# Projection of a hybrid attention block: splits before results, squares a tile ahead, three places for rotation rows

## The chip, the cores and the metric

The kernel runs on one core of one Trainium2 chip. The metric is the device time of one execution in microseconds (us). Two executions of it are told apart when their medians differ by more than the spread of the runs, which is about 0.1% here.

## The reference, cut to what matters

One encoder layer on 2048 tokens of width 1024, in float32. The part at hand is its beginning:

```python
h = rmsnorm(x, g_norm_mix[l])
proj = h @ w_in[l]                      # 1024 x 2304
qa, ka, va, qb, kb, vb = jnp.split(proj, split_at, axis=-1)
qb = partial_rope(qb.reshape(b, s, SWA_HEADS, HEAD_DIM), pos)
kb = partial_rope(kb.reshape(b, s, SWA_KV_HEADS, HEAD_DIM), pos)
oa = neighbourhood_attention(qa, ka, va, na_rpb[l]).reshape(b, s, A_WIDTH)
ob = windowed_gqa_sink(qb, kb, vb, swa_sink[l]).reshape(b, s, B_WIDTH)
o = jnp.concatenate([rmsnorm(oa, g_out_na[l]), rmsnorm(ob, g_out_swa[l])], axis=-1)
x = x + o @ w_out[l]
# a SwiGLU feed-forward with its own norm, and a final norm, follow
```

## The kernel before, in words

Each float32 factor of a product is split into a high and a low part in the format of the fast matmul, and a product is made of three matmuls (high by high, high by low, low by high). The projection runs in two stages, attention and the feed-forward follow.

In the first stage, 16 tiles of 128 tokens are loaded (three buffers), squared and summed by ScalarE, normalised by VectorE into one buffer, transposed on TensorE (turn_tile, 8 small matmuls) and multiplied with the values' columns (value_step, 24 matmuls). ScalarE copies the turned tile's high half out (turn_hi), VectorE makes the low half (turn_lo). For every pair of tiles sums of quarters are formed (turn_copy on ScalarE, turn_sums on VectorE) in a stage buffer hs of seven slices; for the second half of the tokens SyncE stores hs to DRAM (store_sums), and the operands are loaded from there later.

In the second stage the other columns are made with a scheme of seven products in place of eight: 14 groups g (7 column groups for each half b of the tokens) of seven products j, 98 in all, each of 12 matmuls. Step n = 7 g + j. The weights of a group arrive in one of two buffers (load_raw, issued by GpSimd); VectorE forms four sums of them, and ScalarE and VectorE split each product's weights into a ring of six (pair_hi, pair_lo), six steps ahead. ScalarE copies three of the seven banks out (evacuate), VectorE adds others onto them (join). Each group gives four results; ScalarE makes the high and VectorE the low part in one of three stages (result_hi, result_lo), and SyncE stores both. Group 1 of each half is first rotated by VectorE with cosine and sine rows loaded by SyncE (rope, load_rope), and one result of groups 1 and 2 takes a spare buffer. The second half's seven operands are loaded by SyncE (load_op) and split on both engines (split_hi, split_lo) from step 24 on. Eight tiles of output weights are loaded, split and stored along the way (load_out_weights, out_weights_hi, out_weights_lo, store_out_weights).

Nothing schedules this at run time: every engine runs its own list in program order, and semaphores make it wait. So an instruction that waits holds up all that stands behind it on its engine, transfers of SyncE's queue too. The order on each engine is written by hand in the loops over t (tiles) and n (steps), with tables such as HI_AT (the step of a group at which a result is handled), SPLIT_AT and OUT_AT. TensorE needs for product n its weights, and for j = 2, 4 and 5 that ScalarE has copied the bank filled two products before; for j = 6 that VectorE's join of j = 4 is done.

At the end SyncE loads masks and bias rows (load_near), and the first queries, keys and values of attention (first_loads); GpSimd forms biases from masks and rows (make_bias).

## Time and profile before

| | |
|---|---|
| median of 3 runs | 2266.8 us (2265.73 to 2267.71) |
| the profiled execution | 2267.85 us, its span 2266.0 us |
| TensorE busy | 2166.6 us, 96% |
| VectorE busy | 1565.9 us, 69% |
| ScalarE busy | 1012.7 us, 45% |
| GpSimd busy | 243.7 us, 11% |
| mean granted TensorE clock | 0.983 of full speed |

The times of the profile are microseconds from the span's start. PE is TensorE, PEld its weight loads, DVE VectorE, ACT ScalarE, POOL GpSimd, SPq SyncE's queue of transfers. L853 is a line of the kernel. In brackets or behind a bar stands how long an engine was idle before an instruction, and what ended that.

### The profile page before, as it was taken

The page shows a single profiled execution, that of the slowest core. Times are in us where ns is not written, and L with a number is a line of the kernel's source. Part 1 is how long each engine was busy: PE and PEld are TensorE (multiplying, and loading weights), DVE is VectorE, ACT ScalarE, POOL GpSimd, SP SyncE. Part 2 cuts the span into 40 slices and gives each one's busy share as a digit, 9 for nine tenths or more (in the row PEclk, how much of TensorE's full clock was granted, in tenths as well). Part 3 has the DMA queues.
Part 4 walks back from the last instruction along what each step waited for, and adds up shares of the span by engine and source line. Part 5 has one row for each costly group of instructions (what it writes and reads, how often), then busy time and mean ns, then how long its engine had stood idle before and what let it go on. Part 6 is the DMA issues. An engine that isn't in the chain of part 4 may idle for free.

```text
span 2266.0 us, 33068 instructions
## 1 busy us (share of the span) xinstructions
PE 2166.6 (96%) x11168; PEld 1787.7 (79%) x11168; DVE 1565.9 (69%) x2892; ACT 1012.7 (45%) x1967; POOL 243.7 (11%) x275
## 2 busy tenths in 40 slices
PE   7888988969999999999999999999999999999998
PEld 5677766758888888888888888888888888888887
DVE  5466676649988868777666666866666678665676
ACT  5443443448889944344333334433333334131333
POOL 2234100036400000001211111100000000000000
PEclk9989998989999999999999999999999999999999
DMA  6666676899985356665555557623232276353544
GB/s 196 186 192 196 194 243 225 276 246 259 243 219 172 110 190 211 241 219 171 190 172 190 172 190 251 222 89 121 89 121 89 103 287 235 112 181 110 178 152 157
DMA packets 267558, 419.34 MB, mean 185 GB/s; under 512 B 15242, under 2 KB 157074, under 8 KB 260896
## 3 DMA queue, kind: packets, MB, share of 16 engines
q1 hardware_dynamic: 254736, 378.20, 52.2%
q0 software_dynamic: 10240, 30.48, 4.5%
q10 hardware_dynamic: 2448, 8.91, 1.3%
q8 instruction: 79, 1.29, 0.2%
q14 instruction: 55, 0.45, 0.1%
HBM read 264.70 MB, written 156.04 MB: 186 GB/s over the span
## 4 chain that ended last, share of the span: by engine, by line
PE 80%; DVE 7%; DMA 5%; issue 3%; ACT 3%; SPq 1%; DVEq 0%; ACTq 0%
PE late_psum L2334 11%; PE late_psum L2336 11%; PE late_psum L2335 11%; PE late_psum L2360 6%; PE late_psum L2361 6%; PE late_psum L2362 6%; PE late_psum L1278 4%; PE late_psum L1255 3%; PE late_psum L1676 3%; PE late_psum L1678 3%; PE late_psum L1677 3%; PE late_psum L853 2%; PE late_psum L855 2%; PE late_psum L854 2%; PE late_psum L1243 2%
## 5 line engine op out<-in xcount | busy, mean ns | idle before, releaser
L2334 PE MATMUL late_psum<-ff_h,ff_ring 128*128 128x512 f32 x1232 | 479.6, 389 | 1.3 <-DVE ff_acts L2195 1.2
L2336 PE MATMUL late_psum<-ff_h,ff_ring 128*128 128x512 f32 x1232 | 479.3, 389 | 0.0
L2335 PE MATMUL late_psum<-ff_h,ff_ring 128*128 128x512 f32 x1232 | 479.3, 389 | 0.0
L2334 PEld LDWEIGHTS late_psum<-ff_h,ff_ring 128*128 128x128 f32 x1232 | 231.2, 188 | 50.1 <-DVE ff_acts L2195 2.1
L2335 PEld LDWEIGHTS late_psum<-ff_h,ff_ring 128*128 128x128 f32 x1232 | 231.2, 188 | 48.0
L2336 PEld LDWEIGHTS late_psum<-ff_h,ff_ring 128*128 128x128 f32 x1232 | 231.2, 188 | 47.9
L2360 PE MATMUL late_psum<-ff_d,ff_a 128*128 128x512 f32 x616 | 240.1, 390 | 2.1 <-DVE ff_x L2253 1.4
L2362 PE MATMUL late_psum<-ff_d,ff_a 128*128 128x512 f32 x616 | 239.7, 389 | 0.0
L2361 PE MATMUL late_psum<-ff_d,ff_a 128*128 128x512 f32 x616 | 239.7, 389 | 0.0
L2253 DVE TENSOR_TENSOR ff_x<-late_psum,ff_x 128x512 f32<-128x512 f32 x224 | 153.3, 689 | 118.1 <-PE late_psum L2362 117.5
L2153 DVE TENSOR_TENSOR ff_ring<-ff_raw,ff_ring 128x512 fp32r<-128x512 f32 x176 | 130.1, 740 | 101.2 <-ACT ff_ring L2030 101.2
L1143 ACT ACTIVATE att_probs<-att_neg_scores,att_negmax 128x385 f32<-128x385 f32 (+4 forms) x256 | 161.2, 630 | 29.6 <-DVE att_negmax L1190 28.5
L2153 DVE TENSOR_TENSOR ff_ring<-ff_sums,ff_ring 128x512 fp32r<-128x512 f32 x132 | 96.9, 735 | 112.2 <-ACT ff_ring L2030 111.9
L2045 ACT CAST ff_a<-ff_a 128x768 fp32r<-128x768 f32 (+2 forms) x96 | 81.4, 877 | 205.6 <-DMA ff_a<-acts_scratch 205.5
L2030 ACT CAST ff_ring<-ff_raw 128x512 fp32r<-128x512 f32 x176 | 109.3, 622 | 136.9 <-PE late_psum L2336 135.9
L1255 PE MATMUL late_psum<-ident,att_probs 128*128 128x128 f32 (+1 forms) x816 | 133.2, 276 | 8.7 <-ACT att_probs_turned L1165 4.0
L1165 ACT COPY att_probs_turned<-late_psum 128x384 f32<-128x384 f32 (+2 forms) x256 | 124.6, 488 | 29.3 <-PE late_psum L1255 29.1
L2360 PEld LDWEIGHTS late_psum<-ff_d,ff_a 128*128 128x128 f32 x616 | 115.6, 188 | 27.9 <-issue 2.1
L2362 PEld LDWEIGHTS late_psum<-ff_d,ff_a 128*128 128x128 f32 x616 | 115.6, 188 | 23.9
L2361 PEld LDWEIGHTS late_psum<-ff_d,ff_a 128*128 128x128 f32 x616 | 115.6, 188 | 23.8
L2030 ACT CAST ff_ring<-ff_sums 128x512 fp32r<-128x512 f32 x132 | 81.5, 619 | 113.6 <-PE late_psum L2336 108.2
L1243 PE MATMUL late_psum<-att_k_stack,att_q_stack 128*128 128x384 f32 (+3 forms) x256 | 112.5, 439 | 19.4 <-issue 12.0
(204 smaller groups left out, 4125.8 us busy)
## 6 DMA issues: line engine op xcount, KB each, us to landing
acts_scratch<-ff_acts SPq DMA_DIRECT2D x22, 1792.0 KB, 7.5
ff_a<-acts_scratch SPq DMA_DIRECT2D x24, 960.0 KB, 5.3
ff_raw<-in_w_gate SPq DMA_DIRECT2D x44, 512.0 KB, 3.8
ff_raw<-in_w_up SPq DMA_DIRECT2D x44, 512.0 KB, 3.9
att_q_stack<-qk_scratch SPq DMA_DIRECT2D x64, 256.0 KB, 6.5
ff_d<-down_scratch SPq DMA_DIRECT2D x21, 768.0 KB, 6.8
proj_raw<-in_w_in POOLq DMA_DIRECT2D x14, 1024.0 KB, 8.6
ffn_in_scratch<-mix_h_stage SPq DMA_DIRECT2D x8, 1792.0 KB, 6.2
```

Of the source, the lines that this page charges most:

```text
L1143: nc.scalar.activation(pr[:, i, lo:hi], sn[:, i, lo:hi], ACT.Exp, bias=negmax[:, i:i + 1], scale=-1.0, accum_out=total[:, i:i + 1]).then_i ...
L1243: pe.matmul(out, q, kind.keys(k_st[:, e, 0, :], t), start=True, stop=False)
L1255: last = pe.transpose(tp[0:rows, u % 2, j * P:(j + 1) * P], pr[:, i, c0 + j * P:c0 + j * P + rows], ident[:])
L2030: nc.scalar.copy(ff.ring[m % TURNS][:, 0], weight_of(m)).then_inc(w_hi_done, 1)
L2153: nc.vector.tensor_tensor(ff.ring[m % TURNS][:, 1], weight_of(m), ff.ring[m % TURNS][:, 0], ALU.subtract) \
L2253: nc.vector.tensor_tensor(to, down_bank(e, j), to, ALU.add).then_inc(added, 1)
L2334: pe.matmul(out_bank, whi[:, k], hhi[:, :, k], start=(k == 0 and not onto), stop=False, skip_group_check=onto)
L2335: pe.matmul(out_bank, whi[:, k], hlo[:, :, k], start=False, stop=False, skip_group_check=onto)
L2336: last = pe.matmul(out_bank, wlo[:, k], hhi[:, :, k], start=False, stop=(k == 3), skip_group_check=onto)
L2360: pe.matmul(bank, hi, dhi, start=(i == 0 and not onto), stop=False, skip_group_check=onto)
L2361: pe.matmul(bank, hi, dlo, start=False, stop=False, skip_group_check=onto)
L2362: last = pe.matmul(bank, lo, dhi, start=False, stop=(i == n - 1), skip_group_check=onto)
```

## The change

It changes the order of work in the projection on all engines but TensorE, and moves three pieces of it to other engines. The arithmetic is the same.

- First stage: ScalarE's square is its own step, done a tile ahead, and so are mean and reciprocal on VectorE. Root and normalised tile come first in each turn of the loop. The stage buffer hs is stored in four transfers instead of one, each as soon as its slices are there; ScalarE waits only for the slices that it writes (parts_stored), VectorE for its own (h_stored). The first operands and three weight pairs are split a tile or two earlier.
- Second stage: within a step ScalarE splits weights and operands ahead of results. Results are handled one to two steps later, their low halves one step after the high ones.
- Rotation rows have three places of their own; the three first are loaded at once, the last by ScalarE into the place of the first.
- Five operand loads of the second half are issued by ScalarE, from step 42 on, and its splits stand at other steps.
- GpSimd forms the weight sums of groups 7, 8 and 9; the others stay on VectorE, two of them earlier.
- Output weights come every five steps from 53 on, instead of every four from 59.
- Bias rows and the first mask are loaded at steps 78, 83 and 87, the two other masks at 97 behind the first loads of attention, which are issued at steps 91, 93 and 94. Biases of the first kind wait for their own rows alone. ScalarE waits in attention, ahead of its fifth step, for the last store of stage 2 (last_stage_stored).

```diff
-    SPLIT_AT_TILE = {13: (0, 2), 14: (0, 3), 15: (0, 4)}
-    SPLIT_AT = {0: (0, 6), 24: (1, 1), 31: (1, 0), 45: (1, 2), 46: (1, 3), 47: (1, 4), 49: (1, 5), 51: (1, 6)}
+    LATE_OPS, OP_SLOTS = PER_G * HALF_GROUPS - PER_G - 2, range(2, SEVEN)
+    SPLIT_AT_TILE = {12: (0, 2), 13: (0, 3), 14: (0, 4), 15: (0, 6)}
+    PAIR_AT_TILE = {11: 0, 12: 1, 13: 2}
+    SPLIT_AT = {26: (1, 1), 33: (1, 0), 46: (1, 2), 48: (1, 3), 49: (1, 4), 51: (1, 5), 52: (1, 6)}
+    SUMS_BY_POOL, SUMS_AT = (7, 8, 9), {1: 2}
+    PAIRS_AT = {n: (n + RING,) for n in range(PRODUCTS - RING)}
+    PAIRS_AT.update({0: (4, 5, 6), 1: (), 2: (), 3: (7,), 4: (8, 9), 5: (10, 11)})
...
-    HI_AT = {ROPED: (2, 5, 6, 8), VALUES: (1, 6, 5, 9)}
-    ROPE_AT = (1, 4, 5, 7)
-    order = sorted(((PER_G * g + HI_AT.get(kind_of(g), (1, 4, 5, 6))[i], g, i) for g in range(G) for i in range(4)))
+    HI_AT = {ROPED: (3, 6, 7, 9), VALUES: (3, 7, 6, 9)}
+    ROPE_AT = (2, 5, 6, 8)
+    ROPE_SLOT = (0, 1, 2, 0)
+    order = sorted(((PER_G * g + HI_AT.get(kind_of(g), (3, 5, 6, 7))[i], g, i) for g in range(G) for i in range(4)))
...
     def store_sums(u):
+        sp.wait_ge(h_copied, 2 * u + 2)
+        sp.dma_start(sums_dram[5, :, u - 4], hs[:, 5]).then_inc(parts_stored, 16)
         sp.wait_ge(h_summed, 4 * (u + 1))
-        sp.dma_start(sums_dram[:, :, u - 4].rearrange("o p c -> p o c"), hs[:]).then_inc(h_stored, 16)
+        sp.dma_start(sums_dram[2:5, :, u - 4].rearrange("o p c -> p o c"), hs[:, 2:5]).then_inc(h_stored, 16)
+        sp.dma_start(sums_dram[6, :, u - 4], hs[:, 6]).then_inc(h_stored, 16)
+
+    def store_parts(u):
+        sp.wait_ge(h_copied, 2 * u + 1)
+        sp.dma_start(sums_dram[0:2, :, u - 4].rearrange("o p c -> p o c"), hs[:, 0:2]).then_inc(parts_stored, 16)
...
+    def load_rope(eng, b, i):
+
+        side, half = SIDES[i]
+        if i == 3:
+            eng.wait_ge(roped, 4 * b + 1)
+        elif b == 0:
+            eng.wait_ge(v_done, NT)
         else:
-            sp.wait_ge(prod_done, HOME_FREED[o])
-        sp.dma_start(hc[:, o, 1].bitcast(F32), sums_dram[o].rearrange("p q c -> p (q c)")).then_inc(h_in[o], 16)
+            eng.wait_ge(prod_done, PER_G * HALF_GROUPS)
...
-    OUT_AT = {59 + 4 * k: k for k in range(KT)}
+    OUT_AT = {53 + 5 * k: k for k in range(KT)}
...
+            if g - 1 in SUMS_BY_POOL:
+                last_weight_sum(pool, g - 1)
+            if g in SUMS_BY_POOL:
+                first_weight_sums(pool, g)
+                middle_weight_sum(pool, g)
...
             nc.scalar.copy(v_st[:, t % 2, :], mm[:, t % 4, :]).then_inc(tok_done, 1)
+            if t + AHEAD < NT:
+                root(t + AHEAD)
+            if t + 5 < NT:
+                load_x(t + 5)
             if t + 2 < NT:
                 turn_hi(t + 2)
-                if t + 5 < NT:
-                    load_x(t + 5)
                 turn_copy(t + 2)
-            if t + AHEAD < NT:
-                root(t + AHEAD)
+            if t + AHEAD + 1 < NT:
+                square(t + AHEAD + 1)
...
             if n < PRODUCTS:
                 evacuate(n)
+            if n - LATE_OPS in OP_SLOTS:
+                load_op(act, n - LATE_OPS)
+            for m in PAIRS_AT.get(n, ()):
+                pair_hi(m)
+            if n in SPLIT_AT:
+                split_hi(*SPLIT_AT[n])
             for r, g, i in results_at(n):
                 result_hi(r, g, i)
-            if n + RING < PRODUCTS:
-                pair_hi(n + RING)
-            if n in SPLIT_AT:
-                split_hi(*SPLIT_AT[n])
+                if kind_of(g) == ROPED and i == 0:
+                    load_rope(act, g // HALF_GROUPS, 3)
...
         for t in range(NT):
+            if t + AHEAD < NT:
+                normed_tile(t + AHEAD)
             if t + 2 < NT:
                 turn_lo(t + 2)
                 if t % 2:
                     turn_sums((t + 2) // 2)
-            if t + AHEAD < NT:
-                normed_tile(t + AHEAD)
+            if t + AHEAD + 1 < NT:
+                mean_tile(t + AHEAD + 1)
...
-            if n + RING < PRODUCTS:
-                pair_lo(n + RING)
-            if n in SPLIT_AT:
-                split_lo(*SPLIT_AT[n])
-            for r, gg, i in results_at(n):
+            for r, gg, i in results_at(n - 1):
                 result_lo(r, gg, i)
             for gg, i in ropes_at(n):
                 rope(gg, i)
-            if j == 2 and g + 1 < G:
-                weight_sums(g + 1)
-            if j == 4 and g + 1 < G:
-                last_weight_sum(g + 1)
+            for m in PAIRS_AT.get(n, ()):
+                pair_lo(m)
+            if n in SPLIT_AT:
+                split_lo(*SPLIT_AT[n])
```

## Rows read from the trace of the kernel before

**Rows 1.** Page, part 1: busy time of TensorE, share of the span.

```profile
PE 2166.6 (96%) x11168; PEld 1787.7 (79%) x11168; DVE 1565.9 (69%) x2892; ACT 1012.7 (45%) x1967; POOL 243.7 (11%) x275
```

**Rows 2.** Stretches: PE, PEld, DVE, ACT, POOL busy us; clock, DMA share, GB/s.

```profile
14.30:146.70 132.40, 114.80 (x496) 92.38 (x497) 70.76 (x114) 59.75 (x109) 31.73 (x63) 0.91 0.57 173
146.70:462.10 315.40, 282.36 (x1193) 228.54 (x1191) 206.62 (x301) 134.22 (x215) 52.43 (x85) 0.95 0.71 228
462.10:503.00 40.90, 20.20 (x131) 16.71 (x131) 19.00 (x71) 18.69 (x49) 16.20 (x15) 0.75 1.06 241
503.00:2266.00 1763.00, 1745.29 (x9336) 1446.91 (x9334) 1264.10 (x2400) 792.91 (x1583) 140.86 (x106) 1.00 0.55 176
```

**Rows 3.** TensorE's waits, 14.3 to 146.7: us in total, times, longest.

```profile
PE late_psum L792 <- DVE x_normed L657: 16.9, 9, 3.4
```

**Rows 4.** Timeline of TensorE: start, duration, instruction, idle before.

```profile
22.38 1.09 PE L792 MATMUL late_psum<-ident,x_normed 128*128 128x128 f32 x8 [0.42 <-ACT proj_h_stage L491]
...
54.24 1.09 PE L792 MATMUL late_psum<-ident,x_normed 128*128 128x128 f32 x8 [1.94 <-DVE x_normed L657]
...
60.66 1.05 PE L792 MATMUL late_psum<-ident,x_normed 128*128 128x128 f32 x8
```

**Rows 5.** Timeline of all engines, 110 to 114 us.

```profile
110.35 1.01 ACT L489 COPY proj_h_stage<-late_psum 128x1024 f32<-128x1024 f32 x1 [3.53 <-DMA proj_in_scratch<-proj_h_stage]
...
111.47 1.29 DVE L632 TENSOR_TENSOR x_turned<-late_psum,x_turned 128x512 fp32r<-128x512 f32 x2 [6.91 <-ACT proj_h_stage L489]
...
113.28 1.28 DVE L657 SCALAR_TENSOR_TENSOR x_normed<-x_tile,rstd,g_mix_rows 128x1024 f32<-128x1024 f32 x1 [0.27 <-ACT rstd L498]
```

**Rows 6.** TensorE's waits, 146.7 to 462.1.

```profile
PE late_psum L853 <- ACT proj_c L540: 22.5, 5, 8.1
PE late_psum L853 <- issue: 6.5, 3, 3.9
PE late_psum L853 <- DVE proj_c L697: 2.1, 3, 1.0
PE late_psum L853 <- DVE proj_ring L671: 1.9, 1, 1.9
```

**Rows 7.** Timeline of TensorE within a product.

```profile
149.44 0.39 PE L853 MATMUL late_psum<-proj_h_first,proj_ring 128*128 128x512 f32 x1
...
150.12 0.39 PE L853 MATMUL late_psum<-proj_h_first,proj_ring 128*128 128x512 f32 x1
```

**Rows 8.** Timeline of SyncE's queue and VectorE around the first rotation.

```profile
192.03 1.01 SPq L294 DMA_DIRECT2D rope_rows<-in_rope  x2
197.76 0.01 DVE L711 LOAD_MASK_SELECT rope_swapped<-proj_c  x1 [6.63 <-DMA rope_rows<-in_rope]
```

**Rows 9.** Timeline of ScalarE: split of an operand.

```profile
303.88 1.89 ACT L513 CAST proj_h_second<-proj_h_second 128x2048 fp32r<-128x2048 f32 x1
```

**Rows 10.** Groups by line and shape: busy us, mean ns, idle before.

```profile
L667 DVE TENSOR_TENSOR proj_h_second<-proj_h_second 128x2048 fp32r<-128x2048 f32 x7 | 16.0, 2292 | 7.0 <-ACT proj_h_second L513 7.0
...
L1121 POOL TENSOR_TENSOR bias<-near_mask,rel 128x512 f32<-128x512 f32 x24 | 32.3, 1379 | 2.0 <-DVE att_negmax L1190 2.0
```

**Rows 11.** Timeline while GpSimd forms bias rows, 460 to 463 us.

```profile
459.94 3.38 POOL L1121 TENSOR_TENSOR bias<-near_mask,rel 128x384 f32<-128x384 f32 x3
...
461.07 1.39 DVE L727 TENSOR_TENSOR stage_lo<-proj_c,stage_hi 128x512 fp32r<-128x512 f32 x1 [0.78 <-ACT stage_hi L568]
...
462.96 0.69 DVE L729 SCALAR_TENSOR_TENSOR stage_lo<-late_psum,stage_hi 128x512 fp32r<-128x512 f32 x1 [0.49 <-ACT stage_hi L568]
```

**Rows 12.** Timeline at the seam to attention.

```profile
474.17 0.63 PE L1243 MATMUL late_psum<-att_k_stack,att_q_stack 128*128 128x352 f32 x1 [11.96 <-issue]
...
499.07 0.76 PE L1243 MATMUL late_psum<-att_k_stack,att_q_stack 128*128 128x480 f32 x1 [5.18 <-DMA att_q_stack<-qk_scratch]
```

**Rows 13.** Line 308, the seven operand loads of 1 MB: time to landing.

```profile
DMA to landing us min/median/max: 5.9/10.0/14.0
```

**Rows 14.** Timeline of ScalarE: output weights.

```profile
370.83 1.15 ACT L576 ACTIVATE w_out_parts<-w_out_raw,g_out 128x1024 fp32r<-128x1024 f32 x1 [5.59 <-DMA w_out_raw<-in_w_out]
```

More of the change, by code:

```diff
@@ L257, in results_split, with last_stage_stored, near_arrived @@
         eng.wait_ge(res_lo, LOWS)
-    def near_arrived(eng):
-        eng.wait_ge(near_in, 16 * len(near_parts))
+    def last_stage_stored(eng):
+        eng.wait_ge(stored[2], max(v for r, v in stored_by.items() if r % STAGES == 2))
+    def near_arrived(eng, kind):
+        if kind == 0:
+            eng.wait_ge(near_in, 48)
+        else:
+            eng.wait_ge(near_masks_in, 32)
     def out_weights_stored(eng):
@@ L348, in store_out_weights, with first_loads, later_loads @@
         sp.dma_start(out_dram[k], out_parts[:].bitcast(F32)).then_inc(out_stored, 16)
-    OUT_AT = {59 + 4 * k: k for k in range(KT)}
+    OUT_AT = {53 + 5 * k: k for k in range(KT)}
     def load_near(part):
         dst, src = near_parts[part]
-        sp.dma_start(dst, src).then_inc(near_in, 16)
-    def first_loads(att):
-        sp.wait_ge(prod_done, PRODUCTS - 6)
-        for slot in range(STAGES):
-            sp.wait_ge(stored[slot], max(v for r, v in stored_by.items() if r % STAGES == slot and order[r][1] < G - 2))
-        att.load_q(att.near, 0, 0)
-        sp.wait_ge(prod_done, PRODUCTS - 4)
-        att.load_k(att.near, 0, 0)
-        att.load_k(att.near, 0, 1)
-        sp.wait_ge(prod_done, PRODUCTS - 3)
-        for half in range(2):
-            sp.wait_ge(v_stored[half], 32 * NT)
-            sp.wait_ge(v_stored_by_pool[half], 32 * NT)
-        att.load_v(att.near, 0, 0)
-        att.load_v(att.near, 0, 1)
+        sp.dma_start(dst, src).then_inc(near_in if part < 3 else near_masks_in, 16)
+    def first_loads(att, turn):
+        sp.wait_ge(prod_done, PRODUCTS - SEVEN + (1, 3, 4)[turn])
+        if turn == 0:
+            for slot in range(STAGES):
+                sp.wait_ge(stored[slot], max(v for r, v in stored_by.items() if r % STAGES == slot and order[r][1] < G - 2))
+            att.load_q(att.near, 0, 0)
+        if turn == 1:
+            att.load_k(att.near, 0, 0)
+            att.load_k(att.near, 0, 1)
+        if turn == 2:
+            for half in range(2):
+                sp.wait_ge(v_stored[half], 32 * NT)
+                sp.wait_ge(v_stored_by_pool[half], 32 * NT)
+            att.load_v(att.near, 0, 0)
+            att.load_v(att.near, 0, 1)
+    def later_loads(att):
         att.load_k(att.near, 0, 2)
         att.load_q(att.near, 0, 1)
-    def later_loads(att):
         att.load_v(att.near, 0, 2)
@@ L409, in sync @@
                 sp.wait_ge(table_made, 16 * (2 + 8 * NAH))
-                for part in range(3):
-                    load_near(part)
-            if n == 91:
+                load_near(0)
+            if n in (83, 87):
+                load_near({83: 1, 87: 2}[n])
+            for r, g, i in results_at(n - 1):
+                store_result(r, g, i)
+            if n == 91:
+                first_loads(att, 0)
+            if n == 93:
+                first_loads(att, 1)
+            if n == 94:
+                first_loads(att, 2)
+            if n == 97:
                 out_weights_stored(sp)
@@ L584, in scalar @@
         load_x(2)
-        root(0)
-        root(1)
+        for n in range(2):
+            square(n)
+            root(n)
         turn_hi(0)
@@ L592, in scalar @@
         load_x(4)
+        square(2)
         root(2)
@@ L740, in vector @@
         dve.wait_ge(table_loaded, 1)
-        normed_tile(0)
-        normed_tile(1)
+        for n in range(2):
+            mean_tile(n)
+            normed_tile(n)
         turn_lo(0)
@@ L776, in vector @@
                 rope(gg, i)
[L777 to L780 removed]
+            for m in PAIRS_AT.get(n, ()):
+                pair_lo(m)
+            if n in SPLIT_AT:
+                split_lo(*SPLIT_AT[n])
+            if g + 1 < G and g + 1 not in SUMS_BY_POOL:
+                if n == SUMS_AT.get(g + 1, PER_G * g):
+                    first_weight_sums(dve, g + 1)
+                if j == 2:
+                    middle_weight_sum(dve, g + 1)
+                if j == 5:
+                    last_weight_sum(dve, g + 1)
             if n - 2 in OUT_AT:
@@ L1112, in make_bias @@
                 pool.wait_ge(shifted, UNITS * r + 8 * freed)
-            elif kind == 1:
-                proj.all_read(pool)
-                proj.results_split(pool)
+            else:
+                proj.near_arrived(pool, kind)
+                if kind == 1:
+                    proj.all_read(pool)
+                    proj.results_split(pool)
             for e in range(2):
```

161 lines of the change are left out of this document (81 added, 80 removed).

## Prediction

> **What bounds the kernel now.** I read the page's engine shares first: TensorE is busy 96% of the span [rows 1]. A change on other engines can only pay where TensorE idles or is granted half its clock, so I read the busy time by stretch next [rows 2]. After 503 us TensorE is busy 1745.3 of 1763.0 us at full clock; nothing touched by the diff can gain there. Before it lie three stretches: 132.4 us of normalising, turning and the first values, 315.4 us of products, and 40.9 us at the seam to attention. The third view gives TensorE's waits in each [rows 3, 6], the fourth the pace when it doesn't wait [rows 4, 7].
>
> First stretch. Two turns that start at 54.24 and 60.66 with no wait between them give 6.42 us for a turn and its 24 matmuls. From the turn at 22.38 there are 14 such pairs and one value step of 24 matmuls at 0.227 us (5.45): 22.4 + 14 x 6.42 + 5.45 = 117.7 us, where products start now at 146.7. So 29.0 us are lost. Waits for the normalised tile explain 16.9 [rows 3]. The other 12.1 are clock: the stretch has a mean grant of 0.91 [rows 2], that is 2.4 GHz with spells at 1.2 GHz behind the longer waits, and 0.09 x 132.4 is 11.9.
>
> Products. Three matmuls take 0.68 us [rows 7], 12 take 2.72, 98 products 266.8, and 16 small transposes about 2: 268.7. The stretch takes 315.4, so 46.7 are lost: 33.0 in waits [rows 6] and 13.7 at half clock (by the grant, 0.05 x 315.4 = 15.8 at most).
>
> Seam. TensorE ends its products at 462.1, waits 12.0 us and later 5.2, and is past the last long wait at 499.07 [rows 12]; DMA share is 1.06 meanwhile [rows 2].
>
> **Part 1, norms and squares.** The chain stands in [rows 5]. ScalarE waits 3.53 us for the store of the stage buffer, copies (1.01), and only then does VectorE make its low halves (1.29), after which mean, reciprocal and root follow and the normalised tile starts at 113.28, done at 114.56; TensorE has waited 3.4 for it. The change squares a tile ahead, puts root and normalised tile first after the value copy, and lets the copy wait only for its own two smaller stores. The normalised tile then needs: the turn before it read (about 1.1 us behind the value step), then 1.28. That is 2.4 of 6.5 us until the next turn, so the wait goes. What comes later instead are the low halves and sums: value copy and turned halves (three at about 0.55, half the 1.01 of the wide copy), the copy (1.0) and the low halves (1.3) end some 4.8 us after the value step, behind a turn of 1; they are wanted at 7.6, when the next turn and the next value step are over. VectorE's work for two tiles is 2 x 1.28, eight operations at 0.65 (two take 1.29 [rows 5]) and 0.6 of small ones: 8.4 of 12.8 us. The slack of 2.8 us is also what hides a late store. I take 27 of the 29.0; bounds 20 (a third of the copies still wait for a store) and 29. The first product waited 1.9 us for a weight half; four operands and three pairs are now split a tile earlier, and that wait is part of the next sum.
>
> **Part 2, order in the products.** Now ScalarE's result copy stands before its weight halves, so a result that isn't joined or rotated stops the ring. Moving results to steps 3, 5, 6, 7, one step behind the join, and VectorE's low halves to the step after, removes that. What it costs is a later store: the shortest reuse of a stage goes from high half at step 3 to high half at step 7, leaving 4 x 2.72 less about 4.4 for lows and issue, 6.5 us for the store to land, and then ScalarE can still be 3.8 us late before TensorE misses a bank copy. No row shows how long these stores take. Loads of 1 MB took 5.9 at best, 10.0 in the median and 14.0 at worst [rows 13]; a pair of stores is half a megabyte, so I take under 6.5 and cost it at nothing. At 10.0 it would still be covered, at 14.0 not.
>
> **Part 3, rotation rows.** The second pair of table rows is issued at 192.03 and VectorE stands 6.63 us until 197.76 [rows 8], and TensorE's wait of 8.1, the longest of its kind [rows 6], follows. The same happens in the second half. Three buffers are now loaded before any rotation, and only the fourth use is reloaded, five products (13.6 us) ahead, by ScalarE. Both waits go.
>
> **Part 4, operands and weight sums.** A split is 1.9 us on ScalarE [rows 9] and 2.29 on VectorE [rows 10]. Between steps 46 and 52 VectorE has 5 splits x 2.2, 7 pairs, 3 joins and 4 lows x 0.6: 19.4 us of work in seven products of 19.05. Before, four weight sums (4 x 0.6) came on top for the same steps. GpSimd takes them for three groups: 12 sums of 512 columns at 1.38 us [rows 10], 16.6 us of an engine with nothing else to do there; each group's four fit in its 19 us. By my schedule VectorE finishes the last split about when product 55 wants it, and the join before it is 0.7 late. So the three waits of 6.5 in total [rows 6] shrink to about 1.5, clock included 2. The five loads of 1 MB are on ScalarE's queue, first at step 42, one every 2.72 us (its engine loses nothing: issues run beside its copies). With stores and one weight load about 8 MB move in 27 us. A load wanted 10.9 us after issue against a median of 10.0 and a longest above it is thin; I add 2 us [rows 13].
>
> GpSimd's sums have one price more. While GpSimd formed bias rows, a VectorE subtraction with both inputs in SBUF took 1.39 us; the next, of the same width but with a PSUM input, took 0.69 [rows 11]. Twelve such delays of 0.70 are 8.4 us, of 1.38 each 16.6; the offload saves 12 x 0.61 = 7.3. In the seven crowded steps five of them fall: 3.5 to 7 us late, of which most reaches the last two splits. I take 2.5.
> The Trainium skill, page "SBUF — State Buffer", section "Who interferes with whom", says that a VectorE instruction with two SBUF inputs and a GpSimd one that reads SBUF take turns, the later blocked for the whole instruction. The trace agrees as far as one delayed subtraction can; by the rule the sum would be at the upper bound (7 instead of 2.5), by the row at the lower.
>
> **Part 5, output weights.** ScalarE waited 5.59 us for a load two steps ahead of use [rows 14], and TensorE's waits of some 3 us stand behind such places. Loads now stand every five steps; at the tight ones about 6.6 us remain. I leave 1.5 us.
>
> Products together: 46.7 lost now, less 2 + 2 + 2.5 + 1.5 = 8 left: gain 38.7, bounds 22 (half of it stays, because transfers are late) and 46.
>
> **Part 6, seam.** The first attention loads are issued at steps 91, 93 and 94 instead of behind step 95's store, the queries so about 13 us ahead of TensorE's end (step 91 and 2 to 3 us). But masks and three stores (2.8 MB) now go ahead of the later keys and queries. Volume decides: some 6.8 MB behind the end of products at 241 GB/s [rows 2] are 28 us, with the latency of the last 30, until the third query block, where it is 36.9 now [rows 12]. I take 6; bounds 0 and 12. The new wait of ScalarE in front of its fifth attention step is for a store issued 3 to 5 us after the end; behind it stand exponentials of later units, and cover is the wait for keys.
>
> **Sum.** 27 + 38.7 + 6 = 71.7. Profiled execution 2267.85 (span 2266.0), median 2266.8, 1.05 lower: 2266.8 - 71.7 = 2195, taken as 2196.
>
> **Rivals.**
> A. As summed: 2196, its own range 2184 to 2210. For it: each wait has a named cause that the new order takes out. Chance 0.60.
> B. Transfers become the bound. DMA share was 0.71 in the products; the same bytes in 275 us make 0.81, and with part 1 some stretches ask for 300 GB/s. Landings stretch, half of the products' gain goes: 2196 + 23 = 2219. Chance 0.18.
> C. GpSimd's sums block VectorE for whole instructions, splits late, 7 us and some clock: 2206. The rule of the Trainium skill quoted above leads here. Chance 0.12.
> D. The seam gives nothing: 2202. Chance 0.06.
> E. Slower than before: the later stores. If a pair of stores needs over 6.5 + 3.8 = 10.3 us, ScalarE holds TensorE once in each of 14 groups; to eat 71 us it must be 5.4 more, 15.7 us each. The 1 MB loads at their slowest are near that, pairs of 256 KB shouldn't be. 2270 or more: 0.02.
> Left over 0.02 for no visible change.
>
> **Chances and range.** Faster A to D, 0.96; same 0.02 (4.5 us, 0.2%, is about what a measurement of this kernel tells from nothing); slower 0.02. Below 2180 all bounds would have to be good at once; above 2222 lies a good third of B. Range 2180 to 2222.
>
> **What the profile would show.** Right: waits on the normalised tile gone and the first product near 118 to 121; no wait for rotation rows; grant near 1.00 in both stretches; products in 274 to 280 us; third query block 30 us behind. Wrong: VectorE subtractions of 1.4 to 2 us around GpSimd's sums with waits at products 54 and 55 (C); splits, output weights or result copies that wait for transfers (B); the third query block still 37 us behind (D); result copies that wait for stores in each group (E).

## The result and the profile after

The changed kernel takes 2212.92 us (median of four executions, 2211.68 to 2217.22) against 2266.27 for the kernel before on the same chip: ratio 0.977 [0.975, 0.979], 53.4 us faster, where 70.8 were forecast. Its profiled execution took 2214.03 us (span 2212.2, mean grant 0.991), 53.8 less than that of before. The page's first part and the busy time by stretch (columns as in [rows 2]):

```profile
PE 2147.7 (97%) x11168; PEld 1778.0 (80%) x11168; DVE 1566.8 (71%) x2880; ACT 1012.2 (46%) x1967; POOL 267.4 (12%) x287
```

```profile
14.30:115.90 101.60, 101.10 (x496) 84.54 (x497) 74.53 (x118) 61.16 (x111) 31.62 (x63) 1.00 0.71 226
115.90:409.40 293.50, 275.60 (x1193) 225.10 (x1191) 200.71 (x284) 131.60 (x212) 79.51 (x99) 0.98 0.75 241
409.40:446.80 37.40, 19.73 (x116) 15.99 (x116) 17.66 (x59) 17.05 (x43) 13.64 (x12) 0.68 1.05 272
```

Beside [rows 1, 2] this splits the gain. The first stretch shrank from 132.4 to 101.6 us (30.8; forecast 27), the products from 315.4 to 293.5 (21.9; forecast 38.7). The rest follows by the same pair of matmuls in both traces. (Attention works in units, eight to a block of queries: the ninth opens the second block, the seventeenth the third.) Those of the twenty-first unit of attention start 54.02 us earlier, first before, then after:

```profile
506.48 0.47 PE L1243 MATMUL late_psum<-att_k_stack,att_q_stack 128*128 128x480 f32 x1
452.46 0.47 PE L1299 MATMUL late_psum<-att_k_stack,att_q_stack 128*128 128x480 f32 x1
```

The profiled executions as wholes differ by 53.8. So the seam gave 54.0 - 30.8 - 21.9 = 1.3 (forecast 6). The waits of TensorE in the three stretches, answering to [rows 3, 6]:

```profile
PE late_psum L859 <- DVE v_w_lo L722: 0.5, 1, 0.5
PE late_psum L847 <- DVE x_normed L717: 0.3, 1, 0.3
...
PE late_psum L908 <- ACT proj_c L588: 7.8, 2, 6.9
PE late_psum L908 <- DVE proj_c L740: 6.2, 1, 6.2
PE late_psum L908 <- DVE proj_h_second L727: 2.2, 2, 1.6
PE late_psum L908 <- issue: 1.7, 2, 1.3
...
PE late_psum L1299 <- DMA att_q_stack<-qk_scratch: 7.8, 1, 7.8
PE late_psum L1299 <- issue: 6.1, 1, 6.1
PE late_psum L1299 <- DVE stage_lo L775: 3.5, 1, 3.5
```

Of the first stretch 0.8 us of waits is left, at full clock. Most of its turns come faster than the 6.42 us of [rows 4]:

```profile
21.53 1.09 PE L847 MATMUL late_psum<-ident,x_normed 128*128 128x128 f32 x8 [0.29 <-DVE x_normed L717]
27.95 1.04 PE L847 MATMUL late_psum<-ident,x_normed 128*128 128x128 f32 x8
34.29 1.03 PE L847 MATMUL late_psum<-ident,x_normed 128*128 128x128 f32 x8
```

The first two stand 6.42 apart, the next 6.34, and all later ones 6.33 to 6.37; the mean up to the turn at 104.12 is 6.35. The first starts 0.85 earlier than before: 21.53 + 14 x 6.35 + 5.45 = 115.9, where products start. The one pace of 6.42 here begins at a turn behind a wait (0.29), and so did the pair in the trace of before from which 6.42 was taken (1.94 at 54.24).

Among the products TensorE waits 17.9 us, in seven waits. Three of them, 0.60, 1.59 and 0.40, stand at the first products of the second half, which need its operands (2.6). One of 1.28, at 133.68, is at the first product on the last operand of the first half. No wait for rotation rows is left. The other 14.0 (6.93, the 0.89 some 11 us behind it, and 6.22) have one cause, seen in the timeline of SyncE's queue, ScalarE and TensorE:

```profile
284.53 1.50 SPq L349 DMA_DIRECT2D qk_scratch<-stage_hi  x1
286.07 0.93 SPq L349 DMA_DIRECT2D qk_scratch<-stage_lo  x1
286.62 0.39 ACTq L312 DMA_DIRECT2D rope_rows<-in_rope  x1
287.04 0.98 SPq L358 DMA_DIRECT2D w_out_raw<-in_w_out  x1
298.75 1.15 ACT L624 ACTIVATE w_out_parts<-w_out_raw,g_out 128x1024 fp32r<-128x1024 f32 x1 [10.06 <-DMA w_out_raw<-in_w_out]
...
304.61 0.63 ACT L616 ACTIVATE stage_hi<-proj_c 128x512 fp32r<-128x512 f32 x1 [3.20 <-DVE proj_c L762]
305.14 0.57 ACT L588 COPY proj_c<-late_psum 128x512 f32<-128x512 f32 x1
305.76 0.79 PE L908 MATMUL late_psum<-proj_h_second,proj_ring 128*128 128x512 f32 x1 [6.93 <-ACT proj_c L588]
306.36 0.63 PE L909 MATMUL late_psum<-proj_h_second,proj_ring 128*128 128x512 f32 x1
306.78 0.63 PE L910 MATMUL late_psum<-proj_h_second,proj_ring 128*128 128x512 f32 x1
...
362.58 1.15 ACT L624 ACTIVATE w_out_parts<-w_out_raw,g_out 128x1024 fp32r<-128x1024 f32 x1 [6.81 <-DMA w_out_raw<-in_w_out]
365.71 0.80 PE L908 MATMUL late_psum<-proj_h_second,proj_ring 128*128 128x512 f32 x1 [6.22 <-DVE proj_c L740]
```

Read it from the bottom of a block upward. The load of output weights is issued at 287.04, and ScalarE reaches the instruction that needs it at 288.7. The load is there at 298.75, 10.7 us after the issue ended, behind two pairs of stores and a table row. ScalarE works in order: while it stands, the weight halves and the copies of banks behind it stand too, VectorE's joins and rotations wait for those, and TensorE has nothing to do from 298.8. When the load is there, VectorE has to catch up first: ScalarE stands another 3.20 us for a rotated result, and only then copies the bank that TensorE waits for. The same begins with the wait that ends at 362.58.

The granted clock falls to 1.2 GHz inside each of the two waits and stays there for 6.8 us, of which 4.4 and 5.9 lie behind the wait. There matmuls start 0.43 us apart and not 0.227, which costs 2.2 and 2.9 us. (The expectation below counts the whole 6.8 us, 3.4 lost each; the part inside the wait costs nothing more.) So 14.0 + 5.1 = 19.1 of the 24.8 that this stretch (293.5) loses against 268.7. With the waits of 2.6 and 1.28 that makes 22.9; the other 1.9 go back to neither waits nor clock. The first edit below has as much (1.7) at full clock, so the base of 268.7 is some 2 us low.

The seam, in the timeline of SyncE's queue, ScalarE and TensorE, answering to [rows 12]:

```profile
401.79 6.05 SPq L1105 DMA_DIRECT2D att_k_stack<-qk_scratch  x8
...
415.07 1.25 SPq L372 DMA_DIRECT2D near_mask<-in_na_mask  x2
419.90 0.60 ACT L616 ACTIVATE stage_hi<-late_psum 128x512 fp32r<-128x512 f32 x1 [9.66 <-DMA qk_scratch<-stage_lo]
421.27 0.66 PE L1299 MATMUL late_psum<-att_k_stack,att_q_stack 128*128 128x352 f32 x1 [3.50 <-DVE stage_lo L775]
426.19 1.26 SPq L1095 DMA_DIRECT2D att_q_stack<-qk_scratch  x2
434.49 0.77 PE L1299 MATMUL late_psum<-att_k_stack,att_q_stack 128*128 128x480 f32 x1 [7.79 <-DMA att_q_stack<-qk_scratch]
```

The first unit starts 6.3 us behind the end of the products, against 12.1. But the last result copy waits 9.66 us for an older store to leave its stage buffer. That pair of stores is issued at 409.82 and 412.01, behind the early keys and values (401.79 to 409.8). The keys and queries of the next block are issued behind that result and behind the masks, at 422 to 427. The ninth unit starts 25.1 us behind the end of the products, where it was 21.7 (483.80), and the third query block 37.4 (446.83), where it was 37.0. That the seam gave 1.3 all the same is clock: before, the third block begins behind a wait of 5.18 [rows 12] and its first two units start 1.67 us apart; here it begins with no wait in front and they start 0.88 apart.

### The profile page after: what moved, and what is told of

The parts are those of the page before. It is cut to its first block, busy times and chain, and to the rows that moved or that the text cites. A ratio compares the mean times of both kernels' runs of the same rounds, so it can differ in the third digit from the quotient of the medians.

```text
span 2212.2 us, 33085 instructions
## 1 busy us (share of the span) xinstructions
PE 2147.7 (97%) x11168; PEld 1778.0 (80%) x11168; DVE 1566.8 (71%) x2880; ACT 1012.2 (46%) x1967; POOL 267.4 (12%) x287
## 3 DMA queue, kind: packets, MB, share of 16 engines
q8 instruction: 79, 1.29, 0.2%
## 4 chain that ended last, share of the span: by engine, by line
PE 86%; DVE 5%; DMA 4%; issue 2%; ACT 1%; SPq 1%; DVEq 0%; ACTq 0%
PE late_psum L2391 12%; PE late_psum L2392 12%; PE late_psum L2393 12%; PE late_psum L2417 6%; PE late_psum L2419 6%; PE late_psum L2418 6%; PE late_psum L1334 4%; PE late_psum L1311 4%; PE late_psum L908 3%; PE late_psum L909 3%; PE late_psum L910 3%; PE late_psum L1733 3%; PE late_psum L1735 3%; PE late_psum L1734 3%; PE late_psum L1299 2%
```

## The experiments

Each ratio is to the kernel before, run on the same chip; medians are of four executions, with rotation rows of five. The first four ran beside one another on one chip, then the next four on another, then the last four on a third, so times of different chips are best compared by their ratios. The end of the products is counted from here on from the start of their last matmul (409.18 in the changed kernel), 0.2 us earlier than above.

**Output weights used four steps behind their load.** Undoes the cause named above, and nothing else.

```diff
-            if n - 2 in OUT_AT:
-                out_weights_hi(OUT_AT[n - 2])
+            if n - 4 in OUT_AT:
+                out_weights_hi(OUT_AT[n - 4])
```
(and the same for the low halves on VectorE and the store on SyncE)

> The changed kernel, but each tile of output weights is split on ScalarE and VectorE (and stored) four steps behind its load instead of two. Theory T (too short a distance): ScalarE's waits for these loads, 10.06 and 6.81 us, and with them TensorE's waits of 6.93, 0.89 and 6.22 us and two spells at half clock of 6.8 us (3.4 us lost each) go: about 21 us, 2213 to 2192 us. Rival V (the transfers are too slow whatever the distance): the load still lands late or another wait takes its place, under 8 us gained, above 2205 us.

Measured: 2197.44 us (2197.39 to 2198.46), ratio 0.969 [0.968, 0.971], 70.4 less than before, where the changed kernel has 53.4. The kernel with weight sums on VectorE, no different from the changed one in time, took 14.1 us more on this chip, and the pair further down that ran on one chip differs by 13.2. So the edit is worth 13 to 17 us, nearer to theory T's 21 than to V's 8. The stretch of products by busy time, and what is left of ScalarE's waits for these loads:

```profile
116.20:391.50 275.30, 270.37 (x1192) 221.60 (x1191) 196.93 (x284) 131.94 (x212) 76.68 (x99) 1.00 0.79 256
```

```profile
ACT w_out_parts L624 <- DMA w_out_raw<-in_w_out: 3.9, 3, 2.0
```

In the changed kernel the row of ScalarE is 21.5 us, longest 10.1. The products take 275.3 us at full clock, 18.0 less; waits of 4.9 us are left of 17.9. About 1 us comes back at the seam (the twenty-first unit stands 44.4 behind the end of the products, not 43.3). The cause of the two long waits is thereby shown; its size is 18 us of the 19.1 in the stretch, and 1.1 and 0.2 us of waits are still there.

**Before, with the first stage alone.** Splits square and mean off, puts root and normalised tile first, stores the stage buffer in four.

```diff
+            if t + AHEAD < NT:
+                root(t + AHEAD)
...
-            if t + AHEAD < NT:
-                root(t + AHEAD)
+            if t + AHEAD + 1 < NT:
+                square(t + AHEAD + 1)
```

> The kernel before with the first stage of the change alone: squares, means and reciprocals a tile ahead, root and normalised tile first, the stage buffer stored in four parts. Theory: these parts alone take out all waits and half clock of the first stage, first product at about 116 us instead of 146.7, and the rest stays as it was: 30 us gained, 2236 us. Rival: the later stages were waiting for transfers that are now asked for more densely and give a part back: 10 to 20 us gained, 2247 to 2256 us.

Measured: 2237.81 us (2237.33 to 2239.21), ratio 0.987 [0.985, 0.989], a gain of 30.0. The first stretch and the products, and TensorE's longest group of waits among the products:

```profile
14.30:116.60 102.30, 100.93 (x497) 84.39 (x498) 69.22 (x114) 58.89 (x109) 31.63 (x63) 1.00 0.69 224
116.60:432.60 316.00, 282.70 (x1192) 228.95 (x1191) 207.84 (x301) 134.27 (x215) 52.04 (x84) 0.95 0.71 227
```

```profile
PE late_psum L877 <- ACT proj_c L550: 22.5, 4, 8.1
```

The theory's 2236 nearly came. The first stage's 30 us stand by themselves, without the earlier splits of operands and pairs, and the products neither gain nor lose by starting 30 us earlier.

**Before, with the three places for rotation rows alone**, all loaded by SyncE.

```diff
+    ROPE_SLOT = (0, 1, 2, 0)
...
-        for side, half in enumerate((0, 1) if turn == 0 else (1, 0)):
+        for i in ((0, 1, 2) if turn == 0 else (3,)):
```

> The kernel before with three places for the rotation rows alone (three loads ahead, the fourth behind the first rotation, all by SyncE). Theory: TensorE's waits of 8.1 and 7.7 us and the half clock behind them (6.8 and some 7 us of spells, half of it lost) go: 18 to 22 us gained, 2245 to 2248 us. Rival: in the second half splits and late operands hold the rotation anyway, only the first wait goes: 11 us gained, 2255 us.

Measured: 2257.28 us (2253.3 to 2259.28), ratio 0.995 [0.994, 0.997], a gain of 10.6. TensorE's waits for result copies in the products, the longest of them, and what ScalarE did ahead of it:

```profile
PE late_psum L858 <- ACT proj_c L542: 13.6, 6, 5.1
```

```profile
358.57 1.15 ACT L578 ACTIVATE w_out_parts<-w_out_raw,g_out 128x1024 fp32r<-128x1024 f32 x1 [6.04 <-DMA w_out_raw<-in_w_out]
360.24 0.79 PE L858 MATMUL late_psum<-proj_h_second,proj_ring 128*128 128x512 f32 x1 [5.14 <-ACT proj_c L542]
```

The wait of 8.1 us is gone. Where the one of 7.7 was, one of 5.14 stands, and it isn't for rotation rows: ScalarE stands 6.04 us for output weights. So does the second longest, 3.57 at 416.70, behind 6.49 us for another such load. The four others are 0.7 to 1.4. The places alone gave 10.8 us in the stretch (315.1 to 304.3). The time is the rival's (11), but what holds the second half is output weights and not operands: their loads were too late already in the kernel before.

**Weight sums back on VectorE.**

```diff
-    SUMS_BY_POOL, SUMS_AT = (7, 8, 9), {1: 2}
+    SUMS_BY_POOL, SUMS_AT = (), {1: 2}
```

> The changed kernel with all weight sums on VectorE, none on GpSimd. Theory S (the offload pays): VectorE has 19.4 us of work plus 2.4 us of sums in seven products of 19.05 us, the operand splits get later, TensorE's waits of 0.6, 1.6 and 0.4 us around the first second-half products grow by 3 to 6 us: 2216 to 2220 us. Rival L (what GpSimd's sums cost VectorE by blocking it is as much as they save): no difference beyond 2 us, 2211 to 2215 us.

Measured: 2211.57 us (2210.43 to 2212.42), ratio 0.975 [0.974, 0.977]: no difference from the changed kernel, rival L. The timeline of the changed kernel shows what each engine does to the other:

```profile
254.24 1.29 POOL L453 TENSOR_TENSOR proj_w_sums<-proj_raw 128x512 f32<-128x512 f32 x1 [7.17 <-DVE proj_ring L731]
254.44 3.24 DVE L727 TENSOR_TENSOR proj_h_second<-proj_h_second 128x2048 fp32r<-128x2048 f32 x1 [0.34 <-ACT proj_h_second L561]
255.61 3.22 POOL L455 TENSOR_TENSOR proj_w_sums<-proj_w_sums,proj_raw 128x512 f32<-128x512 f32 x1
257.60 1.78 DVE L773 TENSOR_TENSOR stage_lo<-proj_c,stage_hi 128x512 fp32r<-128x512 f32 x1
```

A split takes 3.24 us in place of 2.29 [rows 10], a subtraction 1.78 in place of 0.69, and GpSimd's own sum 3.22 in place of 1.29. The ends fit turns: the sum ends at 255.53, and 2.29 from there is 257.82, where the split ends at 257.68; 1.29 from 257.68 is 258.97, where the next sum ends at 258.83; 0.69 from there is 259.52, where the subtraction ends at 259.38. A group of VectorE from 150 to 290 us, first with GpSimd's sums, then (second fence) without:

```profile
L731 DVE TENSOR_TENSOR proj_ring<-proj_raw,proj_ring 128x512 fp32r<-128x512 f32 x28 | 21.7, 782 | 9.1 <-ACT proj_ring L573 9.1
```

```profile
L731 DVE TENSOR_TENSOR proj_ring<-proj_raw,proj_ring 128x512 fp32r<-128x512 f32 x28 | 19.0, 686 | 8.3 <-ACT proj_ring L573 8.3
```

That is 2.7 us; the seven splits take 17.0 and not 16.0, 1.0 more; the low halves of results, 21 in two groups, go from 684 and 683 ns to 823 and 804, another 2.8. So 6.5 us are lost to save 12 x 0.685 = 8.2, and GpSimd is busy for 22.2 us more (47.12 against 24.92 in the same stretch). The waits of TensorE for operand splits were 0.60, 1.59 and 0.40 with GpSimd, and 2.18 and 1.02 without.

**The last group's results two steps earlier.**

```diff
-    order = sorted(((PER_G * g + HI_AT.get(kind_of(g), (3, 5, 6, 7))[i], g, i) for g in range(G) for i in range(4)))
+    order = sorted(((PER_G * g + HI_AT.get(kind_of(g), (3, 5, 6, 7) if g < G - 1 else (1, 4, 5, 6))[i], g, i)
+                    for g in range(G) for i in range(4)))
```

> The changed kernel with the results of the last group alone handled at the steps of before (1, 4, 5, 6 instead of 3, 5, 6, 7), so that the store of its first result stands ahead of the attention loads in SyncE's queue. Theory Q (the last result waits 9.66 us for a stage whose store is queued behind 4 MB of attention loads, and the later keys and queries wait behind that result's own store): TensorE's wait of 3.5 us goes, later keys and queries are issued some 4.6 us earlier, the wait of 7.8 us shrinks: 4 to 8 us gained, 2205 to 2209 us. Rival W (the volume of transfers alone sets when the third query block is worked on): under 1.5 us, 2211 to 2213 us.

Measured: 2214.41 us (2212.34 to 2218.1), ratio 0.978 [0.976, 0.980]: no difference, rival W. TensorE's wait of 3.5 us is gone and the next one, for queries, took it over (7.79 before):

```profile
433.28 0.76 PE L1299 MATMUL late_psum<-att_k_stack,att_q_stack 128*128 128x480 f32 x1 [11.84 <-DMA att_q_stack<-qk_scratch]
```

**The first, fourth and fifth together** (output weights four steps behind, sums on VectorE, last results earlier).

> The changed kernel with three edits together: output weights used four steps behind their load, the last group's results at the steps of before, all weight sums on VectorE. If they add up (15.5 and 0 to 1.5 us measured for the first and third, 4 to 8 expected for the second): 2189 to 2194 us. If the seam is bound by volume: 2196 to 2198 us.

Measured: 2201.95 us (2199.96 to 2202.25), ratio 0.971 [0.969, 0.973], above both expectations and some 4.5 us more than the first edit alone on another chip, with intervals that overlap. The traces have the difference: the products take 278.3 us and not 275.3, and the twenty-first unit stands 45.5 behind them (44.4). In the products a wait of 2.3 us for a result copy is new, behind a result's high half that waited 5.25 us for its stage's store. At the seam the ninth unit stands 28.0 us behind (26.4). What each of the two added edits has in it wasn't taken apart.

**The same, with the keys and queries of the next blocks issued a step ahead of the last results.**

```diff
+            att.load_k(att.near, 0, 2)
+            att.load_q(att.near, 0, 1)
```
(in the loads of step 94, and no longer behind the last store)

> As the kernel with the three edits, and besides the third portion of keys and the second query block are loaded right behind the first values (step 94), ahead of the masks and of the last three results' stores. Theory Q: with a stage's store queued ahead the last result isn't held up, the ninth unit's wait for queries goes, but those stores land later: 2 to 5 us gained against the three edits. Rival W: the bytes up to the third query block are the same, no difference beyond 1.5 us; and if the last results' stores are held up behind the added 1.5 MB, the early units wait again and it is slower by 2 to 4 us.

Measured: 2203.51 us (2201.09 to 2205.45), ratio 0.973 [0.971, 0.975]: no gain, rival W. TensorE no longer waits for queries, but for turned probabilities, mainly twice (7.30 and 5.35 us). The first of the two goes back to a store, the second to masks:

```profile
416.05 0.48 ACT L1220 COPY att_probs_turned<-late_psum 128x384 f32<-128x384 f32 x1 [6.67 <-DMA qk_scratch<-stage_lo]
416.67 0.45 PE L1311 MATMUL late_psum<-ident,att_probs 128*128 128x128 f32 x1 [7.30 <-ACT att_probs_turned L1220]
419.79 1.27 POOL L1176 TENSOR_TENSOR bias<-near_mask,rel 128x512 f32<-128x512 f32 x1 [36.06 <-DMA near_mask<-in_na_mask]
```

ScalarE's first copy of turned probabilities stands behind the wait for the last store of stage 2, which the change put in front of its fifth attention step. In the changed kernel that wait is covered by the wait for queries; with queries early it stands open, 6.67 us, and TensorE behind it. The second, at 429.40, stands behind scores that waited for GpSimd's biases, and those for the masks, which are now last. Whichever of keys, queries, masks and results is sent last is the one waited for.

**The first edit with the old order within a step:** results ahead of weight halves on ScalarE, lows and stores in the same step, and the old steps.

```diff
-    HI_AT = {ROPED: (3, 6, 7, 9), VALUES: (3, 7, 6, 9)}
-    ROPE_AT = (2, 5, 6, 8)
+    HI_AT = {ROPED: (2, 5, 6, 8), VALUES: (1, 6, 5, 9)}
+    ROPE_AT = (1, 4, 5, 7)
...
```

> The changed kernel with output weights used four steps behind their load (2197.4 us measured), and the order of before within a step: results ahead of the weights' halves on both engines, at the steps of before (HI_AT, ROPE_AT), low halves and stores in the same step. Rotation places, operand loads and first stage stay as changed. Theory O (splits first is what keeps the ring full): TensorE's waits behind result copies that aren't joined or rotated come back, as the 1.0 to 5.1 us ones in the kernel with rotation places alone: 10 to 20 us slower, 2207 to 2217 us. Rival P (with rotation rows, operands and output weights in time the order costs nothing): within 3 us, 2195 to 2200 us.

Measured: 2212.73 us (2211.36 to 2215.04), ratio 0.977 [0.975, 0.979], 15.3 us more than the first edit (16.5 by the ratios), theory O. The products take 288.7 us and not 275.3, with these waits of TensorE:

```profile
PE late_psum L908 <- ACT proj_c L588: 8.8, 6, 2.2
PE late_psum L908 <- issue: 5.5, 3, 3.6
```

The six of the first line are for bank copies. The three of the second, 1.38, 3.65 and 0.43, stand at the first products of the second half, whose splits the old order puts behind results. So Part 2's order is worth some 15 us once rotation rows and output weights are in time.

**The changed kernel again, beside the three below.**

> The changed kernel itself, unaltered, on the chip on which the next three run, so that they have a common base. 2211 to 2215 us.

Measured: 2211.23 us (2210.44 to 2213.14), ratio 0.976 [0.974, 0.977].

**Output weights four steps behind, sums on VectorE.**

> The changed kernel with output weights used four steps behind their load and all weight sums on VectorE, the seam untouched. Theory L (GpSimd's sums save VectorE about what they cost it by blocking it): within 2 us of the kernel with the output weights alone, 2195 to 2199 us. Rival S (the offload pays once the output weights no longer hide it): 3 us or more slower, above 2200 us.

Measured: 2198.07 us (2198.02 to 2199.67), ratio 0.970 [0.968, 0.971], 13.2 us less than the changed kernel beside it and the same as the first edit, theory L. GpSimd's sums are worth nothing here either.

**Output weights every four steps, masks before the results.** This frees the end of the queue: the last two masks are loaded at step 88.

```diff
-    OUT_AT = {53 + 5 * k: k for k in range(KT)}
+    OUT_AT = {53 + 4 * k: k for k in range(KT)}
...
-            if n == 97:
+            if n == 88:
```
(and the weights used three steps behind their load)

> The changed kernel with output weights loaded every four steps from 53 on and used three steps behind their load, and with the two late masks (1.3 MB) loaded at step 88 instead of 97, ahead of the attention loads. Theory W (the seam takes as long as its transfers): 1.3 MB less behind the products' end at the 291 GB/s measured there are 4.5 us: TensorE is at its ninth unit some 21 us behind the end instead of 25 to 26, and with the output weights' 15 us 2193 us. Rival X (the same bytes crowd the last products instead: three steps are too short or result stores land late): waits of 3 us and more come back among the products, 2198 to 2206 us.

Measured: 2206.41 us (2205.8 to 2208.48), ratio 0.974 [0.972, 0.975], 4.8 us less than the changed kernel beside it, and short of theory W (2193): rival X. TensorE's waits among the products, then at the seam:

```profile
PE late_psum L908 <- DVE proj_c L740: 6.9, 1, 6.9
PE late_psum L908 <- ACT proj_c L588: 5.4, 3, 3.5
...
PE late_psum L1299 <- DMA att_q_stack<-qk_scratch: 4.5, 1, 4.5
PE late_psum L1299 <- DVE stage_lo L775: 2.7, 1, 2.7
```

The ninth unit now stands 18.4 us behind the products (25.0 in the changed kernel beside it) and the twenty-first 35.9 (42.9): the 7 us of the seam were there to be had. But the products take 292.3 us, against 290.8 beside it: at three steps, with a load every four, output weights are late again (ScalarE waits 5.88 us for one at 363.05).

**The same, with sums on VectorE, last results and next keys earlier.**

> As the kernel with the masks early, and besides the last group's results at the steps of before, the third keys and second queries at step 94 and all weight sums on VectorE. Theory W: with masks out of the way neither biases nor queries hold the ninth unit, TensorE is there 16 to 19 us behind the products' end: 2188 to 2192 us. Rival X: result stores queue behind more loads and hold the early units, no better than the masks alone, 2193 to 2203 us.

Measured: 2207.79 us (2204.01 to 2209.24), ratio 0.973 [0.972, 0.975]. That is above both expectations. The ninth unit is at 17.1 us, the twenty-first at 38.0 (35.9 without these edits): nothing more at the seam, and the products unchanged at 291.8. Here too ScalarE stands 5.01 us in front of that step for the last store of stage 2, and TensorE waits 5.70 behind it.

## Why the prediction was right and wrong

**In sum.** The forecast was 2196, the time 2213. It lies inside the range of 2180 to 2222, but outside the 2184 to 2210 of the case with a chance of 0.60: the range held because it reached to case B, not because the sum did. (B's 2219 is 23 more; half of the 38.7 of the products, as it says, would be 19.4 and 2215.) Of the 17.7 us of missing gain (71.7 less 54.0), the products lack 16.8 and the seam 4.7, and the first stage gave back 3.8. In the products Part 5 cost 17.6 more than priced and Part 4 3.9 less; the wait of 1.28 for the last operand of the first half and the base that is 1.9 low were in no term. The total missed by no more than Part 5 alone because Parts 1 and 4 were wrong the other way, by 3.8 and 3.9.

**Part 1 held.** 27 us were forecast and 30.8 came; 30.0 by the run with this part alone. The bound of 29 was too low: it took the pace of a turn (6.42) and the start at 22.38 from the trace of before as fixed. The start had a wait of 0.42 us for the stage buffer in front of it [rows 4]. The pace was read from a turn that stood behind a wait of 1.94, which costs some 0.07 us at its start; without waits a turn takes 6.35. (The 13.7 us that the working puts down to half clock in the products before are some 11 by the spacing of the matmuls; the rest is the base that is low.)

**Part 2 held, and is worth more than its price of nothing says.** No wait of TensorE among the products goes back to a later store, rival E's mechanism, in the changed kernel; ScalarE does wait for stages, 10.1 us in five waits, and that is covered; what goes back to a stage's store is the wait of 3.5 at the seam, behind a copy that stood 9.66 us. With the old order the first edit loses 15 us.

**Part 3 held as to these waits, but not as a gain of its own.** In the old order the places bring 10.6 us and not both long waits: where the second was, late output weights hold TensorE for 5.14.

**Part 4 held in cause, and less came.** Two terms of 2 and one of 2.5 were forecast; the three waits for the second half's operands come to 2.6 without half clock. Rival C was right about the duration of a blocked instruction and wrong about the end. In the Trainium skill, page "SBUF — State Buffer", section "Who interferes with whom", two such instructions take turns, and the later one is blocked for the whole of the other. The trace agrees, for a subtraction of 512 columns (1.78 us beside a sum, 0.69 alone), for a split of 2048 that starts 0.2 us behind a sum of 1.29 and ends 0.95 late, and for GpSimd's next sum, begun beside the split, which takes 3.22: each ends within 0.15 us of where it would by turns. The delays eat 6.5 of the 8.2 us that the offload saves. The predicted 2.5 us of loss by it isn't there; without GpSimd the waits for splits are 3.2 us, with it 2.6.

**Part 5 failed: "At the tight ones about 6.6 us remain. I leave 1.5 us".** This term measured 19.1 in the stretch, 18.0 of which went with the first edit. The working had the right place, and left about 6.6 us to a distance of two steps, which is 5.4 us of products, although the row beside it, a load two steps ahead of use, showed a wait of 5.59 [rows 14], and the 1 MB loads had a median of 10.0 [rows 13]. The load landed after 10.7, with two pairs of stores ahead of it, and ScalarE was at its instruction 0.7 us behind the issue. Of ScalarE's 10.06 us TensorE was covered for 3.1, of its 6.81 us at 362 for 0.6: weight halves, bank copies and high halves stand behind the one waiting instruction, and the joins and rotations of VectorE behind those. That is rival B in one place: "some transfers late", not the volume as such, for with four steps the products run at a DMA share of 0.79 and lose 7 us in all.

**Part 6 failed as rival D says: the seam gives next to nothing.** Volume decides, as the working has it, but the gain was counted for the loads that were moved earlier, and the end depends on the one that is sent last. The first unit came earlier (6.3 us behind the products, not 12.1), the ninth later (25.1, not 21.7). What is sent last sets it: with masks early the seam is 7 us shorter; with keys and queries early and masks late it isn't. TensorE's wait of 3.5 us was for a stage buffer, Part 2's later store met at the seam, and in no term here; taking it away gained nothing, since the wait for queries grew from 7.79 to 11.84. The new wait in front of the fifth attention step was priced at cover, and cover it has in the changed kernel. Where queries come early it has none: it then costs TensorE 7.30 and 5.70 us, which the timelines give as one reason why the two runs with early queries gained nothing at the seam. No run took that wait out.

**Open.** That half a megabyte needs 10.7 us when the DMA share over the stretch is 0.75 is in part the queue at that moment: the share is 0.96 from 285 to 291 us, with GpSimd's megabyte of weights (issued at 282.04), stores and table rows ahead, and 2.8 MB move between the issue and the landing. Why the share is only 0.53 from 292 to 297, with the load still on its way, wasn't settled. The output weights four steps behind together with early masks weren't tried; by the runs above that might be worth up to 7 us more, if the products stay at 275. Nor were early masks and queries without ScalarE's wait for the last store. Why the first, fourth and fifth edit together lose some 4 us was read from their timeline alone.

## What to carry to other kernels

A load that an in-order engine waits for needs a distance taken from landings in the queue as loaded there, if copies that free the matmuls' banks stand behind it: landings took about 10 us, two steps gave 5.4 and four give 10.9, and those two steps were worth 13 to 17 us. At a seam that is bound by volume, what paid was to send something before the crowd; moving one transfer past another only changed which was last. And additions moved from VectorE to GpSimd saved next to nothing here, where VectorE had two-input work in SBUF to do. Before a wait is put down to the kind that was expected there, look at what the releasing engine itself waited for: twice here it was another load or store.

## What the runs showed of the hardware

- Two-input instructions on SBUF slowed each other on VectorE and GpSimd, both ways: 2.29 to 3.24 us and 0.69 to 1.78 on VectorE, 1.29 to 3.22 on GpSimd, each ending within 0.15 us of where it would if the two took turns. Twelve sums of 512 columns took GpSimd 21.9 us (1.40 to 2.22 each by group means), where [rows 10] gave 1.38 each.
- A 512 KB load behind two pairs of 256 KB stores and a table row took 10.7 us from the end of its issue until it was used; the 1 MB operand loads of the changed kernel took 9.7 in the median.
- A store waited behind loads that were issued before it: a stage buffer came free 9.66 us late in the first microseconds of the seam, where the core moves 272 GB/s at a DMA share of 1.05.
- The granted clock stayed full through waits of 0.4 to 1.6 us among the products. Inside those of 6.93 and 6.22 us it went to 1.2 GHz and stayed there for 6.8 us each, 4.4 and 5.9 of them behind the wait (matmuls 0.43 us apart and not 0.227; 2.2 and 2.9 us lost). With no wait over 1.6 us left there, the products of the first edit ran at 1.00.
